# Two chained transformer blocks on one core: small rows moved to another DMA queue, one set of condition columns moved to an earlier block, ten weight loads issued before the mixer ends

## The reference, cut to what matters

```python
silu_c = silu(c)                                     # c: one row of 1024
mod = silu_c @ ada_w[i] + ada_b[i]                   # 6 x 1024 "condition" values a layer
sh_t, sc_t, ga_t, sh_c, sc_c, ga_c = split(mod, 6)
hn = rms_norm(x, norm_tm_g[i]) * (1 + sc_t) + sh_t
x = x + ga_t * rwkv7_mix(hn, ...)                    # layer 0: three 1024 x 1024 projections, a chunked
                                                     # recurrence of 16 heads, an output product w_o
hn = rms_norm(x, norm_cm_g[i]) * (1 + sc_c) + sh_c
x = x + ga_c * hier_moe(hn, ...)                     # 32 experts, two of them for each token
```

## Time and profile before

| | us |
|---|---|
| median of three runs | 2578.49 (2577.26 to 2581.31) |
| the profiled execution's own time | 2577.54 |
| its span, from first to last instruction | 2575.8 |
| PE busy | 2256.2 (88%) |
| DVE busy | 860.0 (33%) |
| ACT busy | 414.0 (16%) |

### The profile page before, as it was taken

The page is one execution under the profiler, slowest core; times in us unless marked ns, Lnnn a source line. Parts: engine busy times, 40 slices in busy tenths (PEclk is TensorE's granted clock), DMA queues, the critical chain, the costliest instruction groups (busy, mean ns, idle before and its releaser), DMA issues. The chain is left out here.

```text
span 2575.8 us, 40145 instructions
## 1 busy us (share of the span) xinstructions
PE 2256.2 (88%) x17289; PEld 1331.2 (52%) x17289; DVE 860.0 (33%) x1701; ACT 414.0 (16%) x757; POOL 22.2 (1%) x114
## 2 busy tenths in 40 slices
PE   5979999689988999978987999878986999878986
PEld 3759888354437667744433555334432555434432
DVE  5875775631114111523112341122113341122113
ACT  1023332010000000411000133010001133010001
POOL 0000000000000000000000000000000000000000
PEclk7989999789998999989999999979998999979998
DMA  9800000879995664155997433546997433546995
GB/s 375 315 1 4 3 3 3 333 304 420 421 416 198 227 213 165 49 228 230 420 420 316 150 117 128 191 189 269 420 421 300 150 118 129 184 189 268 421 420 218
DMA packets 138912, 602.15 MB, mean 234 GB/s; under 512 B 33832, under 2 KB 36968, under 8 KB 83952
## 3 DMA queue, kind: packets, MB, share of 16 engines
q1 hardware_dynamic: 126480, 591.64, 58.5%
q10 hardware_dynamic: 12000, 7.88, 1.1%
q0 software_dynamic: 256, 0.02, 0.0%
HBM read 598.43 MB, written 1.05 MB: 233 GB/s over the span
## 5 line engine op out<-in xcount | busy, mean ns | idle before, releaser
L2225 PE MATMUL ps<-store 128*32 128x512 f32 (+1 forms) x2816 | 323.5, 613 | 30.0 <-DMA store<-in_w_exp_up 14.3
L2801 PE MATMUL ps<-store,x_features 128*128 128x512 f32 x704 | 322.8, 602 | 3.9 <-PEq L731 3.9
L394 PE MATMUL ps<-store 128*128 128x512 f32 x480 | 213.2, 605 | 11.0 <-PEq L731 7.9
L2225 PEld LDWEIGHTS ps<-store 128*32 128x32 f32 x2816 | 90.2, 113 | 255.5 <-issue 255.5
L2801 PEld LDWEIGHTS ps<-store,x_features 128*128 128x128 f32 x704 | 128.1, 192 | 135.5 <-issue 133.4
L2243 PE MATMUL ps<-store 128*32 128x512 f32 (+1 forms) x1408 | 160.2, 595 | 36.0 <-DVE store L2340 36.0
L2183 PEld LDWEIGHTS ps<-store 128*128 128x128 f32 x1408 | 160.5, 192 | 41.5 <-issue 33.5
L2335 DVE TENSOR_TENSOR store<-ps,store 128x256 f32<-128x256 f32 x44 | 18.7, 425 | 481.4 <-ACT store L2287 481.4
L2183 PE MATMUL ps<-store 128*128 128x128 f32 x1408 | 168.9, 277 | 4.7 <-DVE store L2314 4.7
L424 PE MATMUL ps<-x_features,store 128*128 128x256 f32 x768 | 169.8, 384 | 2.5 <-PEq L731 2.5
L2255 PE MATMUL ps<-store 128*128 128x512 f32 x352 | 163.0, 605 | 0.0
(11 more groups left out here) (408 smaller groups left out, 2291.8 us busy)
## 6 DMA issues: line engine op xcount, KB each, us to landing
store<-in_moe_w_gate SPq DMA_DIRECT2D x64, 1024.0 KB, 18.7
store<-in_moe_w_up SPq DMA_DIRECT2D x64, 1024.0 KB, 20.5
store<-in_moe_w_down SPq DMA_DIRECT2D x64, 1024.0 KB, 23.0
store<-in_w_exp_gate SPq DMA_DIRECT2D x64, 1024.0 KB, 19.0
store<-in_w_exp_up SPq DMA_DIRECT2D x64, 1024.0 KB, 21.1
store<-in_w_exp_down SPq DMA_DIRECT2D x64, 1024.0 KB, 23.2
store<-in_ada_w SPq DMA_DIRECT2D x48, 1024.0 KB, 13.5
store<-in_w_in SPq DMA_DIRECT2D x40, 1024.0 KB, 5.0
```

The costliest lines, as they stand in the source:

```text
L394: mm = pe.matmul(k.ps[:, set_ * 4 + tile * 2 + h, 0:n], xT[:, s, tile * P:(tile + 1) * P], w[:, kk, c0:c0 + n], start=(s == 0), stop=(s == ...
L2225: mm = pe.matmul(v3(k.ps[w * CAP:(w + 1) * CAP, 6, :], 2, F), xe[:, q % 2, s, w], both[:, :, s * F:(s + 1) * F], start=(s == 0), stop=(s = ...
L2801: mm = pe.matmul(k.ps[:, 2 * (j % 2) + tile, :], x, row[:, 0:HALF], start=(s_ == 0), stop=(s_ == K8 - 1))
```

## The change

Three parts.

**Opening.** Of the fifteen small loads behind the positions ACT keeps two (`columns[:2]`: the bias of layer 0's condition and the gain of its first norm), on semaphores of their own. The other thirteen go out on SP after the third unit. DVE's angles wait for the positions only; its shift and scale wait for ACT's two loads; the thirteen are waited for at the end of DVE's program.

**Columns.** `condition_columns` of the first sum of `first1` moves from the norm block to the output-product block, behind the release of the fourth unit; the norm block keeps the second sum's.

**Ten units.** In the mixer's block SP gets a program: it waits for the last outputs of both directions and for the last gate products, then issues ten units. The planner keeps slots 2 and 3 out of those ten, so they take slots 0, 1 and 4 to 11, and the last two of `first1` take 2 and 3.

```diff
+WHILE_FINISHING = 10
@@ make_core
-            pair = min(ring[::2], key=lambda at: max(k.last[at:at + 2]))
+            late = 2 if name in ("rwo", "first1") and len(k.slots) - k.starts["rwo"] < WHILE_FINISHING else None
+            pair = min(ring[::2], key=lambda at: (at == late, max(k.last[at:at + 2])))
@@ opening_phase
-    n_early = 16 * (len(columns) + len(b.early))
+    small = (*columns[2:], *b.early)
+    n_early = 16 * len(small)
@@ opening_phase, sync
+            issue(k, sp, n0 + 3)
+            for dst, src in small:
+                sp.dma_start(dst, src).then_inc(k.early_landed.sem, 16)
             ahead(k, sp, n0 + 8)
@@ opening_phase, vector
-                    vec.wait_ge(k.early_landed.sem, k.early_landed.at(n_early + 16))
+                    vec.wait_ge(k.lora_landed.sem, k.lora_landed.at(16))
                     link(vec.tensor_copy(posf, pos))
...
+            vec.wait_ge(k.small_landed.sem, k.small_landed.at(32))
             vec.wait_ge(k.ada_made.sem, k.ada_made.at(2))
...
             link(vec.tensor_scalar(k.cos[:, :, :], k.cos[:, :, :], -2.0, 1.0, MUL, ADD))
+            vec.wait_ge(k.early_landed.sem, k.early_landed.at(n_early))
@@ opening_phase, scalar
-                          allow_slow_non_contiguous=True).then_inc(k.early_landed.sem, 16)
-            for dst, src in columns[:3]:
-                act.dma_start(dst, src).then_inc(k.early_landed.sem, 16)
+                          allow_slow_non_contiguous=True).then_inc(k.lora_landed.sem, 16)
+            for dst, src in columns[:2]:
+                act.dma_start(dst, src).then_inc(k.small_landed.sem, 16)
...
-            for dst, src in (*columns[3:], *b.early):
-                act.dma_start(dst, src).then_inc(k.early_landed.sem, 16)
@@ to_features_phase, tensor
-                for m, acc in enumerate(first):
-                    condition_columns(k, pe, acc, 4, m)
+                condition_columns(k, pe, first[1], 4, 1)
@@ residual_phase, tensor
                 pe.wait_ge(k.ada_read.sem, k.ada_read.at(m + 1))
                 pe.sem_inc(k.used, 1)
+                if m == 3:
+                    condition_columns(k, pe, first[0], 4, 0)
@@ rwkv_mix_phase
+        @block.sync
+        def _(sp):
+            for z in range(2):
+                reached(sp, k.output_copied[z], 2 * NB)
+                job_made(sp, "gate", z, NB - 1)
+            n = k.starts["rwo"] + WHILE_FINISHING
+            assert not {2, 3} & {at for at, _, _ in k.slots[k.starts["rwo"]:n]}
+            issue(k, sp, n)
```

More of the change, by code:

```diff
@@ L704, in opening_phase @@
     k.router_landed.close(32)
-    k.early_landed.close(n_early + 16)
+    k.early_landed.close(n_early)
+    k.lora_landed.close(16)
+    k.small_landed.close(32)
     k.vec_done.close(3)
```

## The result

The changed kernel takes 2587.72 us (median of 17 runs, 2580.96 to 2592.38), the kernel before, run beside it, 2578.47 us (17 runs, 2572.34 to 2581.76). The ratio is 1.0037, 95% interval 1.0028 to 1.0047. I had forecast 2569.7 us and a range of 2564 to 2577. The profiled execution of the changed kernel took 2589.84 us, its span is 2588.1 us, the mean granted clock 0.936 (before: 2577.54, 2575.8 and 0.939). Single executions of either kernel lie up to 7 us from their median, so stages are compared inside the profiled executions, by the start of the same instruction in both.

What follows compares the result with a forecast made beforehand. It took DVE's 15.5 us opening wait for small rows, and waits around the mixer's end and norm block, as bounds. Opening 3.6 + ten units 0.3 + columns 3.9 = 7.8 us off 2577.54 gave 2569.7; range 2564 to 2577.

Steps and rivals of the forecast that it cites:

- Does it last?: Projection through expert stage: claimed no load comes late (tightest has 2.2 us left), so the opening's 3.6 us is carried.
- The sum: Whole kernel: 3.6 (opening) + 0.3 (ten units) + 3.9 (columns) = 7.8 us off 2577.54, giving 2569.7 us.
- The opening's gain: Opening block: moving thirteen small loads to SP gains 3.6 us; bounds 5.9 and -3.7 (a loss).
- L: Opening: time at which unit 3, SP's fourth, lands; forecast 21.2 us, far end 28.5 with a second stall.
- L + 14.4: Opening: forecast time of DVE's copy when unit 3 lands later than DVE needs it at 19.4; gain 24.8 - L.
- the 12 that I had named as a sign of being wrong: Opening: SP's issues of the small rows taking over 12 us would show the forecast wrong.
- The ten units: Mixer's end and output product: of DVE's 11.1 us wait 0.3 us comes back, the rest becoming a wait for PE.
- The columns: Norm block: sixteen of 32 records leave it, gaining 3.9 us, with 1.2 us of wait staying; other bound 0.
- The rivals: Full opening 2567.4 (0.14), second stall 2577.0 (0.14), slow small rows 2585.6 (0.06), serial fixed cost 2601.2 (0.02), columns unmoved 2573.6 (0.04).
- The slower one, small rows at 102 packets/us: Opening, SP's queue: small rows need 19.5 us, L = 37.1, total 8.1 us slower at 2585.6; chance 0.06.
- The rule of a fixed cost in series: Opening: thirteen loads each paying about 2.0 us serially; L near 44, total near 2592; rival version 2601.2, chance 0.02.
- expert stages of other length: Expert stages: a changed length would show the forecast wrong, since no step of the change touches them.

Runs made afterwards that it cites:

- SP short: Changed kernel with SP issuing 16 units in the opening instead of 20; 2584.25 us (12 runs), ratio 1.0023 to the kernel before.
- bias first and SP short: Changed kernel with gate bias loads ahead of the lora loads, on their own semaphore, and 16 opening units instead of 20; 2574.17 us, ratio 0.9972.
- opening alone: Kernel before with only the opening's part of the change; 2591.12 us (8 runs), ratio 1.0048 to the kernel before.

## Why the prediction was wrong

**The step that failed is "Does it last?".** It asked which load could come late once SP's units are 3.6 us behind, and looked only at SP's own units (the closest, 9.4 us of slack, was indeed in time). It left out the queue beside them. Row 6 had shown that two full queues give packet for packet, and I had used it to say why ACT's rows were slow in the opening. The same row applies to the projection, where ACT issues ten loads from 46 us on into what SP's queue leaves. Before, the gate bias was ready without a wait shown at 102.64, with some 16 us to spare; after it was 13.2 us late. The sum had 0 for it.

**The opening's gain, 3.6 us, had a second hole.** L, the landing of unit 3, was right (21.87 against 21.2), and so was L + 14.4 for the copy (36.38 against 36.3; the gain is 2.86). The mechanism behind L holds too: the thirteen issues took 12.7 us (4.01 to 16.69, 11.8 forecast, and over the 12 that I had named as a sign of being wrong), their packets passed at up to 1,591 in 1 us, and unit 3 landed 5.1 us after its issue into a queue that had run nearly empty (4.8% from 16 to 17 us). Only the stall fell on another row, 5.72 us on the fourth small load. But the gain was carried to the next block as if DVE's chain ended this one. SP's program, longer by the small rows' time, had not been priced to its end: 20 units, the last issued at 45.74. A block ends with its longest program, which the kernel's own description ahead of the prediction says. So the term of 3.6 us was -0.4 at the projection's start. With that end cut off (SP short) the projection starts 3.0 us earlier than in the changed kernel.

**The ten units.** Forecast 0.3, measured 0.1 in the changed kernel and 0.3 to 0.6 in others at the same clock. SP's ten issues are through at 472.3, before the finishing is at 473.4, and DVE's wait of 11.11 us turned into one of 10.85 us for PE: right.

**The columns.** Forecast 3.9, measured 3.8, with and without the ten units; DVE's wait fell from 5.15 to 1.34 us (1.3 forecast): right.

**The rivals.** None of them happened. The slower one, small rows at 102 packets/us, gives 2585.6, near the result, but for L = 37.1, and L was 21.9: a near number with another mechanism. The rule of a fixed cost in series needed L near 44 or above and is as far off. The mechanism that decided had no chance at all in my list.

**The sum as it was**: +0.4 at the opening, +12.8 at the gate bias, -1.6 on the way to the mixer's end (not caused by an edit), -0.1 and -3.8: +7.7 at L484; at the end 12.3 in the profiled execution and 9 between the medians. What comes on top after 1,400 us has no edit in it and was not traced to a cause; it is also the forecast's own sign of being wrong, expert stages of other length.

## What to carry to other kernels

When small loads go ahead of big ones on a queue, everything behind them is late, and the first to feel it may be the other queue: list every load of the next phases on every queue with its first reader, above all the tiny ones behind large ones, issue those first, and don't let their reader wait on a semaphore that counts the large ones too. Price a program that only issues DMAs to its end, since a block waits for it. And don't put an engine's compute behind a row of issues into a full queue: with two of six loads moved behind it the 1.1 us that this had cost were won back.

## What the runs showed of the hardware

- Two queues with work share the DMA engines packet for packet whatever the packets hold: 283 of 4 KB beside 280 of 256 B in 3 us. The Trainium skill, DMA: Bandwidth & Descriptors (Queues, rings and completion order), has the engines switch between rows of queues at packets, each of several descriptors; the equal counts agree with taking turns, and in bytes it means 1.10 MB against 0.07.
- An issue into such a queue can take 13 to 15 us of the issuing engine's time (13.13 us for 256 KB in SP short, 15.20 in bias first and SP short), where the load of the same size took 0.68 us as the second into ACT's empty queue (46.82 in the changed kernel).
- With the last of SP's 20 opening units landed 4 us later (65.4 against 61.6), ACT's queue beside it emptied 24 to 29 us later: at 110 to 116 us in opening alone and in the changed kernel, not at 87.
- The output product of 64 records took 27.70 us in three executions, 29.24 to 29.57 in ten and 30.74 in one, by when the granted clock rose, which differs between executions of kernels that don't differ there.
